# Expert rows weighted as they leave PSUM and added to the residual in memory by the scatter

## The reference, cut to what matters

```python
def hier_moe(h, rg_w, rg_b, re_w, re_b, e_gate, e_up, e_down):
    ...
    gate = jax.nn.softmax(top_v, axis=-1) * p_grp          # two experts of 32 for each token
    ...
    buf = jnp.zeros((n_blocks * MOE_BLOCK, shp[-1]), t.dtype).at[dest].set(t[tok_sorted])
    ...
        hdn = jax.nn.silu(xb @ e_gate[e]) * (xb @ e_up[e])
        return hdn @ e_down[e]
    ...
    y = ybuf[dest] * gate.reshape(-1)[order][:, None].astype(t.dtype)
    out = jnp.zeros_like(t).at[tok_sorted].add(y)
    return out.reshape(shp)
...
            y = hier_moe(jnp.concatenate([hx2, hc2], axis=1), *moe_p)
            x = x + g2 * y[:, :S]
            ctx = ctx + cg2 * y[:, S:]
```

## Time and profile before

| what | us, or a count |
|---|---|
| median of 3 runs (lowest, highest) | 1892.74 (1892.51, 1894.68) |
| the profiled execution, its own time | 1889.43 |
| its span, from first to last instruction | 1887.6 |
| PE busy | 1640.0 (87%) |
| VectorE, ScalarE, POOL busy | 682.0, 308.5, 227.9 |
| expert phase of layer 0 (first gate product to last eviction) | 541.3 to 1023.8 |
| expert phase of layer 1 | 1389.9 to 1857.9 |
| blocks of 64 rows (evictions on line 1432), layer 0 and layer 1 | 38 and 33 |

### The profile page before, as it was taken

The page is one execution under the profiler, slowest core; times in us unless marked ns, Lnnn a source line. Parts: engine busy times, 40 slices in busy tenths (PEclk is TensorE's granted clock), DMA queues, the critical chain, the costliest instruction groups (busy, mean ns, idle before and its releaser), DMA issues.

```text
span 1887.6 us, 26705 instructions
## 1 busy us (share of the span) xinstructions
PE 1640.0 (87%) x9796; PEld 958.7 (51%) x9797; DVE 682.0 (36%) x1679; ACT 308.5 (16%) x694; POOL 227.9 (12%) x360
## 2 busy tenths in 40 slices
PE   4999999989869999999795899999969979777772
PEld 2455446744646556665353444675546546444441
DVE  2184655653542122222122677563531111111112
ACT  3111126641200000000000401562200000000000
POOL 0000010000012122222121000000012112111111
PEclk9999999999879999999998999999979999999997
DMA  9348146021469999899998603101469999999994
GB/s 383 160 202 349 75 203 274 2 68 56 162 254 426 426 425 427 339 425 425 427 425 335 266 0 158 65 2 34 182 262 426 425 425 426 426 426 426 426 422 181
DMA packets 54328, 530.67 MB, mean 281 GB/s; under 512 B 11896, under 2 KB 12568, under 8 KB 24832
## 3 DMA queue, kind: packets, MB, share of 16 engines
q1 hardware_dynamic: 35744, 487.04, 61.7%
q0 software_dynamic: 15808, 32.39, 4.5%
q10 hardware_dynamic: 2720, 10.49, 1.5%
HBM read 520.87 MB, written 26.28 MB: 290 GB/s over the span
## 4 chain that ended last, share of the span: by engine, by line
PE 61%; DMA 29%; DVE 6%; ACT 2%; issue 1%; POOL 0%; ACTq 0%; POOLq 0%; DVEq 0%
DMA ring<-in_e_down_dram 26%; PE ps L794 22%; PE ps L574 9%; PE ps L606 7%; PE ps L745 7%; PE ps L653 2%; PE ps L668 2%; PE ps L524 2%; PE ps L684 2%; DMA xres<-in_ctx_tokens_dram 2%; PE ps L656 2%; DMA r<-y_dram 1%; PE ps L782 1%; PE ps L728 1%; PE ps L824 1%
## 5 line engine op out<-in xcount | busy, mean ns | idle before, releaser
L794 PE MATMUL ps<-ring,r 128*64 128x256 f32 (+1 forms) x3920 | 534.5, 427 | 80.2 <-DMA ring<-in_e_up_dram 33.7
L794 PEld LDWEIGHTS ps<-ring,r 128*64 128x64 f32 x3920 | 310.1, 138 | 289.7 <-issue 132.4
L794 PE MATMUL ps<-r 128*64 128x256 f32 (+1 forms) x1760 | 238.2, 423 | 31.4 <-DMA r<-in_e_up_dram 14.0
L1412 DVE TENSOR_TENSOR r<-r,ps 128x128 f32<-128x128 f32 x142 | 34.5, 284 | 540.2 <-PE ps L794 540.2
L794 PEld LDWEIGHTS ps<-r 128*64 128x64 f32 x1760 | 141.0, 137 | 120.6 <-issue 54.2
L574 PE MATMUL ps<-r,ring 128*128 128x512 f32 (+1 forms) x480 | 176.7, 527 | 3.7 <-ACT r L1546 2.1
L606 PE MATMUL ps<-ring,r 128*128 128x512 f32 (+1 forms) x384 | 158.1, 566 | 0.0
L745 PE MATMUL ps<-ring,r 128*128 128x512 f32 x320 | 139.2, 594 | 1.4 <-DVE r L1181 1.4
L574 PEld LDWEIGHTS ps<-r,ring 128*128 128x128 f32 x480 | 90.8, 191 | 91.2 <-issue 80.5
L1432 DVE TENSOR_TENSOR r<-ps,r 128x512 f32<-128x512 f32 x71 | 49.1, 692 | 215.3 <-PE ps L794 215.3
L1709 ACT ACTIVATE r<-ps 128x256 f32<-128x256 f32 x71 | 27.3, 384 | 558.9 <-PE ps L794 558.9
(11 more groups left out here) (195 smaller groups left out, 1423.5 us busy)
## 6 DMA issues: line engine op xcount, KB each, us to landing
ring<-in_e_gate_dram SPq DMA_DIRECT2D x44, 2048.0 KB, 41.0
ring<-in_e_up_dram SPq DMA_DIRECT2D x44, 2048.0 KB, 29.4
ring<-in_e_down_dram SPq DMA_DIRECT2D x44, 2048.0 KB
ring<-in_w_mod_dram SPq DMA_DIRECT2D x24, 2048.0 KB, 18.9
r<-in_e_gate_dram SPq DMA_DIRECT2D x20, 2048.0 KB
r<-in_e_up_dram SPq DMA_DIRECT2D x20, 2048.0 KB
r<-in_e_down_dram SPq DMA_DIRECT2D x20, 2048.0 KB
ring<-in_w_in_dram SPq DMA_DIRECT2D x8, 2048.0 KB, 7.9
```

The lines of the kernel that those rows point to most:

```text
L794: mm = pe.matmul(ps[g * B:(g + 1) * B, bank, 0:width], x, w[:, k, g * width:(g + 1) * width], start=(k == first), stop=(k == last), tile_p ...
```

## The change

- The residual goes to memory: behind norm2's statistics POOL stores each `xres` tile to `x_dram` (in layer 1: to `out` itself), ahead of the h2 store of the same tile, and waits for all of them (`x_stored`) before the expert loop.
- The scatter adds (`compute_op=ALU.add`) its rows to `x_dram` or `out`, at the gather's own indices; `list_scatter`, `y_dram`, `combine` and the stores of `out` go.
- The gate is applied in `rows_out`: a second pass of one-hot matmuls gives each block row's gate (`list_row[:, 1]`), after `route_done`; in each block a column of it is copied to `row_now`.
- At layer 0's end ScalarE's queue loads the six tiles of `xres` from `x_dram`, and layer 1's sum of squares starts from there.
- At the start SP loads the tokens by tile, behind constants, tables and conditions and ahead of the weights; the bias rows go behind the fifth chunk, with a semaphore of their own. PE transposes all six tiles ahead of the first modulation step, and ScalarE does its six tiles in one go.
- The routing temporaries move to the last third of `r3` and parts of `r1`, `r2`; `late_slots` change places, so that the eighth piece (the third expert's up) waits for h2 alone and the ninth (its down) for logits and the h2 stores instead of for routing and the first gather.

```diff
-        y_dram = [nc.dram_tensor(f"y_dram{l}", ((2 * (TOK, S)[l] + B) * 2, D // 2), F32, kind="Internal").ap() for l in range(DEPTH)]
+        x_dram = [nc.dram_tensor("x_dram", (TOK * 2, D // 2), F32, kind="Internal").ap(),
+                  out[0].rearrange("t (h n) -> (t h) n", h=2)]
...
-        late_slots = [r2[:, 0:SLOT], r1[:, 0:SLOT], r3[:, 0:SLOT]]
+        late_slots = [r2[:, 0:SLOT], r3[:, 0:SLOT], r1[:, 0:SLOT]]
+        hot_r = r2[:, 4608:6144].rearrange("p (a r) -> p a r", a=2 * NT)
+        hot_q = r1[:, 5120:5888].rearrange("p (a q) -> p a q", a=2 * NT)
...
-            v = r3[:, first:first + n]
+            v = r3[:, 4096 + first:4096 + first + n]
...
-            for layer in range(DEPTH):
-                sp.dma_start(row[:, layer, :], rows[layer].partition_broadcast(P)).then_inc(consts_in, 16)
+            for i in range(NT):
+                src = x[0, i * P:(i + 1) * P, :] if i < XT else ctx_tokens[0, (i - XT) * P:(i - XT + 1) * P, :]
+                sp.dma_start(xres[:, i, :], src).then_inc(tile_in[i], 16)
...
                     load_chunk(layer, j)
+                    if layer == 0 and j == MOD_FIRST:
+                        for m in range(DEPTH):
+                            sp.dma_start(row[:, m, :], rows[m].partition_broadcast(P)).then_inc(rows_in, 16)
...
                     elif n == SLOTS + 1:
+                        sp.wait_ge(h2_ready[layer], tiles)
+                    else:
                         sp.wait_ge(logit_psum[layer], tiles)
                         sp.wait_ge(h2_stored[layer], 16 * tiles)
-                    else:
-                        sp.wait_ge(route_done[layer], 1)
-                        sp.wait_ge(gathered[layer], 16)
...
+                sp.wait_ge(route_done[layer], 1)
                 with sp.Fori(1, NE // HELD) as turn:
...
+                for a in range(n):
+                    pe.wait_ge(onehots[layer], n + a + 1)
+                    mm = pe.matmul(ps[:, 6, 0:B], hot_r[:, a, :], hot_q[:, a, :], start=(a == 0), stop=(a == n - 1))
                 mm.then_inc(list_psum[layer], 1)
...
-                        if 1 <= n < MOD_FIRST:
-                            h1_transposes(0, 2 * n - 2, 2 * n)
+                        if n == 0:
+                            h1_transposes(0, 0, NT)
...
-                for n in range(NT + 2):
+                for n in range(NT + 1):
                     if n < NT:
-                        combine(layer - 1, n)
-                    if n - 1 == 4:
-                        ve.wait_ge(x_done[layer - 1], NT)
-                    if 1 <= n < NT + 1:
-                        scale_tokens(layer, n - 1)
-                    if n >= 2:
-                        modulate(layer, n - 2)
+                        scale_tokens(layer, n)
+                    if n >= 1:
+                        modulate(layer, n - 1)
...
-                for c in range(2):
-                    own(nc.vector.tensor_scalar(value[:, c, :], cst("token")[:, 0:t], float(c * t * P), None, ALU.add))
...
-                own(nc.vector.tensor_scalar(second, ps[:, 2, 0:B], float(t * P + 1), float(-2 * t * P), ALU.is_ge, ALU.mult))
...
-                own(nc.vector.scalar_tensor_tensor(out=list_gather[:, 0:MAXB + 2], in0=twice[:, 0:MAXB + 2], scalar=half2[:, 0:1],
-                                                   in1=second[:, 0:MAXB + 2], op0=ALU.add, op1=ALU.add))
-                nc.vector.tensor_scalar(list_scatter[:, 0:MAXB + 1], twice[:, 0:MAXB + 1], half2[:, 0:1], None,
+                nc.vector.tensor_scalar(list_gather[:, 0:MAXB + 2], twice[:, 0:MAXB + 2], half2[:, 0:1], None,
                                         ALU.add).then_inc(route_done[layer], 1)
+                for a in range(2 * t):
+                    c, i = divmod(a, t)
+                    nc.vector.tensor_scalar(hot_q[:, a, :], cst("slot")[:, 0:B], dest_q[:, c, i:i + 1], gates[:, c, i:i + 1],
+                                            ALU.is_equal, ALU.mult).then_inc(onehots[layer], 1)
...
+                ve.wait_ge(list_psum[layer], 2)
+                own(nc.vector.tensor_copy(list_row[:, 1, :], ps[:, 6, 0:MAXB + 1]))
...
+                        nc.vector.tensor_copy(row_now[:, 1:2], list_row[:, 1, bass.ds(q, 1)]).then_inc(g2_ready[layer], 1)
...
-                    nc.vector.tensor_tensor(y_rows, ps[:, 3, :], g2_block if layer == 0 else g2_rows[:, 0, :],
-                                            ALU.mult).then_inc(y_ready[layer], 1)
+                    nc.vector.scalar_tensor_tensor(out=y_rows, in0=ps[:, 3, :], scalar=row_now[:, 1:2],
+                                                   in1=g2_block if layer == 0 else g2_rows[:, 0, :],
+                                                   op0=ALU.mult, op1=ALU.mult).then_inc(y_ready[layer], 1)
...
-            def combine(layer, i):
...
-                if layer == DEPTH - 1:
-                    for i in range(tiles):
-                        combine(layer, i)
...
-                for i in range(tiles_of(layer)):
-                    ac.dma_start(y_pair[i], y_dram[layer][0:rows, :].rearrange("(c i p h) n -> i p c (h n)", c=2, p=P, h=2)[i]
-                                 ).then_inc(y_loaded[i], 16)
...
+                for i in range(NT):
+                    ac.dma_start(xres[:, i, :], x_dram[layer].rearrange("(i p h) n -> i p (h n)", p=P, h=2)[i]
+                                 ).then_inc(tile_in[i], 16)
...
-            po.dma_start(xres[:, 0:XT, :], x.rearrange("o (i p) n -> p (o i) n", p=P)).then_inc(latents_in, 16)
-            po.dma_start(xres[:, XT:NT, :], ctx_tokens.rearrange("o (i p) n -> p (o i) n", p=P)).then_inc(context_in, 16)
...
                 for i in range(tiles):
+                    po.wait_ge(x_mid[layer], tiles + i + 1)
+                    po.dma_start(x_dram[layer].rearrange("(i p h) n -> i p (h n)", p=P, h=2)[i], xres[:, i, :]
+                                 ).then_inc(x_stored[layer], 16)
...
-                    nc.gpsimd.tensor_copy(idx_scatter[:, :], list_scatter[:, bass.ds(q, 1)]).then_inc(idx_copied[layer], 1)
+                    nc.gpsimd.tensor_copy(idx_scatter[:, :], list_gather[:, bass.ds(q, 1)]).then_inc(idx_copied[layer], 1)
...
-                    po.indirect_dma_start(out=y_dram[layer], in_=y_rows, in_offset=None,
+                    po.indirect_dma_start(out=x_dram[layer], in_=y_rows, in_offset=None,
                                           out_offset=bass.IndirectOffsetOnAxis(ap=idx_scatter[:, 0:1], axis=0),
-                                          bounds_check=4 * tiles * P - 1, oob_is_err=False).then_inc(scattered[layer], 16)
+                                          bounds_check=2 * tiles * P - 1, oob_is_err=False, compute_op=ALU.add).then_inc(scattered[layer], 16)
...
-                if layer == DEPTH - 1:
-                    for i in range(tiles):
-                        po.wait_ge(x_done[layer], i + 1)
-                        po.dma_start(out[0, i * P:(i + 1) * P, :], xres[:, i, :]).then_inc(out_stored, 16)
```

More of the change, by code:

```diff
@@ L312, in hybrid_flow_block @@
         y_psum, y_ready = sems("y_psum"), sems("y_ready")
-        y_loaded = [sem(f"y_loaded_tile{i}_") for i in range(NT)]
-        y_added, x_done, g2_ready = sems("y_added"), sems("x_done"), sems("g2_ready")
-        out_stored = sem("out_stored")
+        tile_in = [sem(f"tile_in{i}_") for i in range(NT)]
+        g2_ready, x_stored = sems("g2_ready"), sems("x_stored")
         xg_cleared = sem("xg_cleared")
@@ L1272, in first_best @@
                     settle()
+                ve.wait_ge(h2_ready[layer], tiles_of(layer))
                 ve.wait_ge(logit_psum[layer], b)
@@ L1380, in route @@
                                             answer[:, :, NG:NG + 1], ALU.mult))
[L1382 to L1384 removed]
+                empty = list_tmp[:, 0:B]
+                twice = list_tmp[:, 2 * B:3 * B]
                 ve.wait_ge(list_psum[layer], 1)
                 own(nc.vector.tensor_scalar(empty, ps[:, 2, 0:B], 0.0, 16384.0, ALU.is_equal, ALU.mult))
[L1387 removed]
                 settle()
@@ L1449, in experts @@
                     rows_out(q)
-            def combine(layer, i):
-                y = y_pair[i]
-                ve.wait_ge(y_loaded[i], 16 * (layer + 1))
-                nc.vector.scalar_tensor_tensor(out=xres[:, i, :], in0=y[:, 0, :], scalar=gates[:, 0, i:i + 1],
-                                               in1=xres[:, i, :], op0=ALU.mult, op1=ALU.add).then_inc(y_added[layer], 1)
-                ve.wait_ge(y_added[layer], i + 1)
-                nc.vector.scalar_tensor_tensor(out=xres[:, i, :], in0=y[:, 1, :], scalar=gates[:, 1, i:i + 1],
-                                               in1=xres[:, i, :], op0=ALU.mult, op1=ALU.add).then_inc(x_done[layer], 1)
-            ve.wait_ge(consts_in, 80)
+            ve.wait_ge(consts_in, 48)
             for layer in range(DEPTH):
-                own(nc.vector.tensor_scalar(nsink[:, layer, :], row[:, layer, 4 * HD:4 * HD + 4], -1.0, None, ALU.mult))
```

(32 more changed lines are left out.)

60 lines of the change are left out of this document (29 added, 31 removed).

## The result

The changed kernel takes 1899.07 us (median of 20 runs, 1894.57 to 1903.32) against 1891.37 us for the kernel before (20 runs, 1887.49 to 1894.68): ratio 1.004, 95% interval 1.0034 to 1.0047. It is slower by 0.4%, 8 us, where I had forecast 12 us faster. The profiled execution took 1900.02 us; its span is 1898.2, where the span before was 1887.6.

A forecast was written before the change was run, and what follows sets the result against it. It took DMA as the bound in the expert phases (layer 0 partly) and PE elsewhere. -9.7 +0.8 +10.5 -4.5 -0.35 +9.5 -18.2 = -12.0 us gave a median of 1880.8 us, range 1862 to 1912.

The forecast's parts named there:

- The start: Up to the first projection: tokens by tile on SP's queue bring it to 40 us instead of 49.71, -9.7 us.
- Layer 0's end: Smaller x loads replace y loads and combines: layer 1's first projection 5.5 us earlier, less 1 for the add, -4.5.
- layer 1's end: The last scatter becomes the last work, without y loads, combines and stores; span ends at 1869.4 us, -18.2 us.
- Routing: Scatter list and one operation removed before the first gather, second one-hots added behind: layer 0 +0.8 us, layer 1 -0.35.
- VectorE per block: In each expert block: one more small copy and an eviction of 0.75 instead of 0.69 us, hidden in idle time: nothing.
- The x stores: Behind norm2: five MB more go out where DMA has room and POOL would wait for h2: nothing.
- The add in the scatter: In both expert phases: reading the destination costs DMA time, +10.5 us in layer 0 and +9.5 in layer 1.
- the one pass: In the scatter: the add costs like one more pass over the same bytes, 9.8 us in layer 1 at 426 GB/s.
- rival B: Expert blocks: the scatter's landing becomes the bound, from 9.9 us on; +26 us, 1907 us; chance 0.20.
- my own sign of being wrong: The accumulating scatter takes more than 10 us to land, or its packets take several times as long.
- w: How much longer the loop eviction, scatter, landing is than PE's 11.81 us per block: 1.5 to 4.6 us, say 3.

The follow-up runs named there:

- kernel 1: The changed kernel with the addition taken out of the scatter, which then overwrites rows (layer 1 routes other tokens): 1879.67 us, ratio 0.9931 to the kernel before.
- kernel 3: The changed kernel with layer 0's lists, scatter, loads and combines as before, so only layer 1 adds in memory: 1882.3 us, ratio 0.9938 to the kernel before.
- kernel 6: The changed kernel with two row buffers in turn and both of POOL's index lists copied ahead: 1896.75 us, ratio 1.0031 to the kernel before.
- kernel 5: The kernel before with every scatter issued twice, the copy to a tensor nobody reads, waits counting both, no addition: ratio 1.0219 to the kernel before.
- kernel 2: The changed kernel with two row buffers in turn, blocks taken in pairs, an odd count ending with an empty block: 1899.62 us, ratio 1.0035 to the kernel before.

## Why the prediction was wrong

*The start* (-9.7). By the runs right: 6 to 11 us. By the trace -6.7 at the first projection (42.3 to 43.5 us in the traces of all seven kernels with this start, 49.1 and 49.7 in those with the old one), since a step of its working was not: I let the weights' transfer bound it, and put ScalarE and the transposes aside as done near 23. They end at 26.8, and the four modulation steps do not wait for chunks but follow each other at 3.6 us. The timeline of the changed kernel:

```profile
26.73 2.15 PE L529 MATMUL ps<-ring,cond 128*32 128x512 f32 x16
29.60 1.05 PE L538 MATMUL ps<-const,mod_row 128*128 128x2 f32 x8 [0.71 <-ACT mod_row L1573]
30.58 1.92 PE L529 MATMUL ps<-ring,cond 128*32 128x512 f32 x16
...
43.05 3.36 PE L579 MATMUL ps<-r,ring 128*128 128x512 f32 x5 [1.56 <-DVE r L984]
```

*Layer 0's end* (-4.5) and *layer 1's end* (-18.2): -4.0 and -17.6. *Routing*: layer 1's -0.35 came out; layer 0's +0.8 is too small for traces that differ by 3 us up to there. *VectorE per block*: right; the 0.75 us of the eviction were the estimate, and kernel 1 shows them free. *The x stores*: nothing is seen of them; kernel 3 has none in layer 0, and takes 495.4 us from the first projection to the first gate product against 493.7.

*The add in the scatter* (+10.5 and +9.5). This step failed, twice. "I take the one pass" counts bytes at 426 GB/s. The mechanism was there: queue 0's share grew to 6.8%, where I said about 6, and the weights came slower. The size was too small: 13.1 us in layer 1 instead of 9.5, and some 14 in layer 0 instead of 10.5 (kernel 6, whose loops are open). The Trainium skill ("Collectives: The Full Stack", section "The bandwidth ceiling: the fold count and why AG ≠ RS ≠ AR") says of ReduceScatter that its add reads two sources where a copy reads one. The trace agrees in direction, 4.1% to 6.8%, but shows no bytes for a second read; and kernel 5 shows that a plain second scatter costs the same.

The other half of the failure is the overlap: the sum let the landing of the scatter hide behind PE's block. That it might not was *rival B of the prediction*, with its place and threshold right: it decides from 9.9 us, the landing was 11.2, and my own sign of being wrong (over 10 us) was met. Its w was 1.5 to 4.6 us, measured 1.0 to 2.0 (12.8 to 13.8 for most blocks, where 11.81 was). Its price was too high: its 26 us stood on top of the forecast's 10.5, so 36.5 in layer 0, and 22.1 were measured between scatters, of which opening the loops gave back only 7. I gave it 0.20, against a margin of 1.6 us that I had worked out myself. The Trainium skill ("DMA: Bandwidth & Descriptors", section "SWDGE vs HWDGE vs iDMA") has the engine alternate between queues at packets. The traces fit that: 68 packets more per scatter and a landing 3.1 us longer under full weights, but only about 2 us longer in an empty queue (4.81 against 2.72 us at layer 0's end). That the turns behind weight packets are the reason was not tried by itself.

With layer 0's measured +23.5 in place of the +11.3 of my sum, it would have come to +0.2: no gain. The rest of the 22.6 us between forecast and spans is layer 1 (4.1), the start (3.0), the 2.1 us that can't be told from chance, and 1.1 at the ends. The range of 1862 to 1912 did hold 1899, since it was drawn wide enough for most of B.

## What to carry to other kernels

Here an indirect transfer that adds cost as much as a second plain scatter of the same rows, in two ways. Beside a saturated weight stream its packets slow the weights (2.8% in layer 1's refills, 11.6 us), whether anybody waits for it or not. And it lands later by more than its bytes say, which matters only inside a loop: subtract the added landing from the loop's slack (here 1.6 us of slack, 3.1 us of added landing), and look at what shares its queue: the gather was late too. A longer wait in a trace doesn't tell how much comes back when the wait is removed: VectorE waited 206 us for scatters, and opening the loops gave back 7. Where the phase is bound by DMA anyway, weigh the transfer against what the tail gives back: in the last layer 17.6 us of tail against 13.6 made it worth having, in the first layer 4 us of seam against 22 did not.

## What was not expected of the hardware

- A plain scatter of the same rows to a second tensor costs as much as the addition: 21.4 and 14.3 us against 22.1 and 13.1.
- POOL's issue of an adding scatter takes 1.60 us, of a plain one 1.03.
- A gather beside adding scatters lands in a median of 10.5 us (560 to 1020 us), where it took 8.5 before and 8.6 beside the plain scatters of kernel 1, although it is itself unchanged.
- An empty block (all indices out of bounds) still costs 5.3 us at the end of layer 1 in kernel 2: 1883.08 to 1888.36 from one adding scatter's issue to the next.
